# Two attention stages of a hybrid decoder block rewritten as deeper software pipelines, and the bodies of the expert loop in another order

## The reference

```
h = RMSNorm(x);  P = h @ W_mix_in        # conv u, B, C | diff q, k, v | memory q
conv   : B * causal_dwconv3(C * u)                                   256 channels
diff   : (softmax(q1 k1/8 + b) - lam * softmax(q2 k2/8 + b)) v       4 heads, causal, v 128 wide
         then RMSNorm per head
memory : softmax(q km/8) vm over 256 fixed tokens                     4 heads of 64
x = x + concat(conv, diff, memory) @ W_mix_out
x = x + MoE(RMSNorm(x))                  # top 4 of 32 experts, clamped SwiGLU, width 1024
out = RMSNorm(x)
```

## Time and profile before

| | |
|---|---|
| time, 3 runs | 2342.4 us median (2339.67 to 2343.84) |
| the profiled execution | 2346.0 us, its span 2344.4 us |
| PE busy | 2175.7 us, 93% |
| DVE busy | 1559.5 us, 67% |
| ACT busy | 1337.9 us, 57% |
| mean granted clock of TensorE | 0.966 |

### The profile page before, as it was taken

One profiled execution on the slowest core, in us unless ns is written; L12 is line 12 of the kernel. 1 busy time (PEld: TensorE's weight loads), 2 busy tenths in 40 slices (PEclk: granted clock), 3 DMA queues, 4 the chain that ended last, 5 costly groups with the idle time before them and its releaser, 6 DMA issues.

```text
span 2344.4 us, 34502 instructions
## 1 busy us (share of the span) xinstructions
PE 2175.7 (93%) x10770; PEld 1797.6 (77%) x10771; DVE 1559.5 (67%) x1640; ACT 1337.9 (57%) x1523; POOL 341.2 (15%) x306
## 2 busy tenths in 40 slices
PE   7999868799499999999999999999999999999993
PEld 6889645599388878877887878778888878888873
DVE  4411256655577658677866888987666888667754
ACT  5111247733366557566746777775556777556654
POOL 1000000012302002011201122121221222122100
PEclk9999979999699999999999999999999999999997
DMA  5111200052679669689968999997776999667854
GB/s 192 55 54 54 90 1 1 25 192 100 200 233 324 218 190 379 229 287 319 379 215 288 361 359 370 362 372 251 226 239 227 322 371 358 222 222 249 302 161 161
DMA packets 265288, 536.93 MB, mean 229 GB/s; under 512 B 14478, under 2 KB 31144, under 8 KB 265132
## 3 DMA queue, kind: packets, MB, share of 16 engines
q1 hardware_dynamic: 248332, 488.26, 58.8%
q0 software_dynamic: 16896, 47.83, 8.4%
HBM read 499.29 MB, written 36.75 MB: 229 GB/s over the span
## 4 chain that ended last, share of the span: by engine, by line
PE 69%; issue 7%; DVE 6%; ACT 3%; DMA 1%; POOL 0%; DVEq 0%; ACTq 0%; SPq 0%; POOLq 0%
PE ps L686 65%; ACT hT_hi L1146 1%; PE ps L911 1%; PE ps L918 1%; DVE work L1400 1%; PE ps L832 1%; DVE hT_lo L1565 1%; DVE w_lo L1554 1%; ACT region_mem L1181 0%; DVE work L1605 0%; DVE hT_lo L1575 0%; ACT hT_lo L1194 0%; DVE weight_ring L1681 0%; DVE slots_between L1554 0%; DVE d_lam L1397 0%
## 5 line engine op out<-in xcount | busy, mean ns | idle before, releaser
L686 PE MATMUL ps<-hT_hi,hT_lo 128*128 128x512 f32 (+1 forms) x4304 | 1399.1, 389 | 12.4 <-DVE hT_lo L1575 12.4
L686 PEld LDWEIGHTS ps<-hT_hi,hT_lo 128*128 128x128 f32 x4304 | 808.5, 189 | 183.3 <-DVE w_lo L1554 18.3
L1146 ACT ACTIVATE hT_hi<-weight_ring 128x2048 fp32r<-128x2048 f32 x417 | 786.9, 1914 | 195.7 <-PE ps L686 142.0
L1554 DVE TENSOR_TENSOR slots_between<-weight_ring,hT_hi 128x2048 fp32r<-128x2048 f32 x245 | 552.7, 2285 | 140.3 <-ACT hT_hi L1146 139.7
L686 PE MATMUL ps<-slots_between,hT_lo 128*128 128x512 f32 x1344 | 527.1, 392 | 0.0
L1554 DVE TENSOR_TENSOR w_lo<-weight_ring,hT_hi 128x2048 fp32r<-128x2048 f32 x140 | 319.5, 2283 | 33.7 <-ACT hT_hi L1146 33.7
L686 PE MATMUL ps<-w_lo,hT_lo 128*128 128x512 f32 (+1 forms) x896 | 336.1, 375 | 0.0
L686 PEld LDWEIGHTS ps<-slots_between,hT_lo 128*128 128x128 f32 x1344 | 254.4, 189 | 54.2
L686 PEld LDWEIGHTS ps<-w_lo,hT_lo 128*128 128x128 f32 x896 | 168.7, 188 | 30.3
L607 POOL DMA_INDIRECT residual_rows<-work,idx_now x48 | 119.0, 2478 | 475.7 <-ACT work L1207 284.8
L601 POOL DMA_INDIRECT work<-normed_rows,idx_far x49 | 86.7, 1770 | 457.4 <-PE ps L911 293.8
(11 more groups left out here) (251 smaller groups left out, 2468.4 us busy)
## 6 DMA issues: line engine op xcount, KB each, us to landing
weight_ring<-in_w_gate_up SPq DMA_DIRECT2D x280, 1024.0 KB, 7.3
weight_ring<-in_w_down SPq DMA_DIRECT2D x140, 1024.0 KB, 5.6
weight_ring<-in_w_mix_in SPq DMA_DIRECT2D x10, 1024.0 KB, 5.9
weight_ring<-in_x SPq DMA_DIRECT2D x8, 512.0 KB, 8.0
weight_ring<-in_w_mix_out SPq DMA_DIRECT2D x4, 1024.0 KB, 5.3
work<-in_x SPq DMA_DIRECT2D x8, 512.0 KB, 4.7
residual_rows<-work SPq DMA_DIRECT2D x8, 512.0 KB, 3.3
normed_rows<-work SPq DMA_DIRECT2D x8, 512.0 KB, 3.6
```

The lines of the kernel that those rows point to most:

```text
L686: return pe.matmul(o, l, r, start=first, stop=last)
L1146: act.activation(w_high_part(u), ring[:, home(u), :], ACT.Copy).then_inc(s["w_high_made"], 1)
L1554: dve.tensor_tensor(w_low_part(u), ring[:, home(u), :], w_high_part(u).bitcast(f32), ALU.subtract)\
```

## The change

Three things, in one version.

1. *Memory stage.* On DVE the normalising of a step goes one step back (maxima of i, then normalise i-1, copy i-2, copy out i-3). PE: scores i, transposes i-2, value product i-3. ACT: copy i-2 first, then the exponentials of i. The loops have one step more.
2. *Diff stage.* DVE: both score maps of j (side 1 first, `SIDES = (1, 0)`), then the difference of j-1. PE: scores j, transposes j-2, value product j-3. ACT: copy j-2, both exponentials of j, then output and square of j-3. The waits between the two stages are put off to where the buffer in question is first used. The square root over the head norms is made in two parts: 28 columns at j = 32, once the squares up to step 29 are through, the last 4 at the end.
3. *Expert loop.* `by_size` tests the other way round, so that the one-block body stands first, the body for two full blocks last.

```
 def by_size(eng, size, body):
-    with eng.If(size > P + 1):
-        with eng.If(size > P + SHORT + 1):
+    with eng.If(size < P + 2):
+        body(("full",))
+    with eng.Else():
+        with eng.If(size < P + SHORT + 2):
+            body(("full", "short"))
+        with eng.Else():
             body(("full", "full"))
-        with eng.Else():
-            body(("full", "short"))
-    with eng.Else():
-        body(("full",))
...
 # PE, diff stage
-            for j in range(NU + 2):
+            for j in range(NU + 3):
                 if j < NU:
-                    for c in range(2):
+                    for at, c in enumerate(SIDES):
                         if j >= 1:
-                            pe.wait_ge(s["ds_read"], 2 * j - 1 + c)
+                            pe.wait_ge(s["ds_read"], 2 * j - 1 + at)
...
-                if 1 <= j <= NU:
-                    n = j - 1
+                if 2 <= j < NU + 2:
+                    n = j - 2
                     pe.wait_ge(s["ds_diff"], n + 1)
...
 # ACT, diff stage
+                if 2 <= j < NU + 2:
+                    n = j - 2
...
                 if j < NU:
                     exponentials(j, 0)
-                if j >= 2:
-                    n = j - 2
+                    exponentials(j, 1)
+                if j >= 3:
+                    n = j - 3
...
+                if j in (NU, NU + 2):
+                    heads = slice(0, NU - HEADS) if j == NU else slice(NU - HEADS, NU)
+                    act.wait_ge(s["ds_sq"], j - 2)
+                    act.activation(o_std[:, heads], o_ssq[:, heads], ACT.Sqrt, ...).then_inc(s["o_std_made"], 1)
...
 # DVE, memory stage: one step back
-                    dve.wait_ge(s["ms_exp"], 4 * (i + 1))
-                    link(dve.reciprocal(m_inv[:, i % 2, :], m_sum[:, i % 2, :]))
+                    j = i - 1
+                    dve.wait_ge(s["ms_exp"], 4 * (j + 1))
+                    link(dve.reciprocal(m_inv[:, j % 2, :], m_sum[:, j % 2, :]))
...
 # DVE, diff stage
                 if j >= 2:
-                    dve.wait_ge(s["ds_turned"], j - 1)
+                    dve.wait_ge(s["ds_turned"] if c == 0 else s["ds_diff"], j - 1)
...
                 if j < NU:
                     scores_read(j, 0)
+                    scores_read(j, 1)
                 if j >= 1:
                     difference(j - 1)
-                if j < NU:
-                    scores_read(j, 1)
```

More of the change, by code:

```diff
@@ L766, in _ @@
             pe.wait_ge(s["proj_dve"], NG // 2)
-            for i in range(NT + 2):
+            for i in range(NT + 3):
                 if i < NT:
@@ L785, in _ @@
                     last.then_inc(s["ms_turned"], 1)
[L786 to L787 removed]
+                if i >= 3:
+                    j = i - 3
                     pe.wait_ge(s["ms_t_act"], j + 1)
@@ L816, in _ @@
                         last.then_inc(s["ds_done"], 1)
-                if j >= 2:
+                if 2 <= j < NU + 2:
                     n = j - 2
+                    pe.wait_ge(s["ds_diff"], n + 1)
+                    if n >= 1:
+                        pe.wait_ge(s["ds_t_act"], n)
+                    else:
+                        pe.wait_ge(s["ms_t_act"], NT)
+                        pe.wait_ge(s["ms_t_dve"], NT)
+                    for b in range(n // HEADS + 1):
+                        last = pe.transpose(ps[:, 4 + b // 4, P * (b % 4):P * (b % 4) + P], wk[:, 2 * (n % 2), P * b:P * b + P], ident[:, :])
+                    last.then_inc(s["ds_turned"], 1)
+                if j >= 3:
+                    n = j - 3
                     i, h = divmod(n, HEADS)
@@ L822, in _ @@
                         pe.wait_ge(s["ds_out"], n - 1)
+                    else:
+                        pe.wait_ge(s["ms_out"], NT)
                     for b in range(i + 1):
@@ L825, in _ @@
                     last.then_inc(s["ds_av"], 1)
-                if 1 <= j <= NU:
-                    n = j - 1
[L828 to L836, removed]
+            pe.wait_ge(s["ds_t_act"], NU)
             pe.wait_ge(s["wo_split"], 16)
@@ L1047, in _ @@
             act.activation(lam[:, 2:4], lam[:, 0:2], ACT.Exp).then_inc(s["lam_exp"], 1)
-            for i in range(NT + 1):
+            for i in range(NT + 2):
+                if i >= 2:
+                    j = i - 2
+                    act.wait_ge(s["ms_turned"], j + 1)
+                    if j >= 2:
+                        act.wait_ge(s["ms_av"], j - 1)
+                    act.activation(wk[:, 2 + j % 2, 0:512], ps[:, 4, :], ACT.Copy).then_inc(s["ms_t_act"], 1)
                 if i < NT:
@@ L1077, in exponentials @@
                     .then_inc(s["ds_exp"], 1)
-            for j in range(NU + 2):
+            for j in range(NU + 3):
+                if 2 <= j < NU + 2:
+                    n = j - 2
+                    nb = n // HEADS + 1
+                    act.wait_ge(s["ds_turned"], n + 1)
+                    if n >= 2:
+                        act.wait_ge(s["ds_av"], n - 1)
+                    act.activation(wk[:, 4 + n % 2, 0:P * nb], ps[:, 4:6, :].rearrange("p b n -> p (b n)")[:, 0:P * nb], ACT.Copy)\
+                        .then_inc(s["ds_t_act"], 1)
                 if j < NU:
                     exponentials(j, 0)
-                if j >= 2:
-                    n = j - 2
+                    exponentials(j, 1)
+                if j >= 3:
+                    n = j - 3
                     i, h = divmod(n, HEADS)
```

61 lines of the change are left out of this document (24 added, 37 removed).

## The result

| | median of 4 runs | range |
|---|---|---|
| kernel before | 2343.1 us | 2339.67 to 2345.58 |
| changed kernel | 2271.45 us | 2267.76 to 2272.37 |

A forecast was written before the change was run, and what follows sets the result against it. Expert loop bound by PE, attention stages by engines waiting for each other in turn. Terms -14 - 24 - 3 - 10 = -51 took 2346.0 to 2295.0, less 3.6 for the median: 2291 us, range 2276 to 2316.

The forecast's parts named there:

- D: Expert loop: reordering the bodies removes four of PE's five long idle times, -10 us, bounds -16 and +16.
- B: Diff stage: reading both maps before the previous step's difference brings steps to their busiest engine, -24 us, bounds -15 and -30.
- A: Memory stage: normalising one step back removes DVE's wait for exponentials, -14.0 us, bounds -5 and -17.
- C: Joint to the e stage: splitting the root takes table load and norm out of the chain, -3 us, bounds 0 and -4.
- the 1.5 and the 0.5: Memory stage: charges of 1.5 us for the longer loop and later last products, 0.5 us for the low clock at the start.
- a full clock: First twelve diff steps: at full clock ACT's 27.0 us is the bound, 30 us with joints, -11.4 us.
- the low-clock bound: First twelve diff steps: if the clock stays low, PE's busy 35.11 us is the bound, -6.3 us.
- The longer drain: Diff stage: filling and draining the longer pipeline, with one value product put ahead of the last, costs +1.5 us together.
- 1: Short diff steps and memory stage: the clock stays low, gains shrink to -8 and -19, 2302 us; chance 0.15.
- 2: Diff stage: side 0's read, waiting for transposes of step j-2, replaces the removed wait, 22 us back, 2313 us; chance 0.10.
- 3: Expert loop: the idle times only change place and the reordering gives 0, 2301 us; chance 0.12.
- 4: Expert loop: every one-block item pays for its two jumps, 79 us at 3.60 each, 2380 us; chance 0.05.

The follow-up runs named there:

- bodies_only: The kernel before with only the bodies of the expert loop in the new order: 2325.7 us, ratio 0.9908.
- sides_0_1: The changed kernel with side 0 read first in the diff stage: 2289.7 us, ratio 0.9760.
- after_pad64: The changed kernel with the expert loop shifted by 32 instructions in PE's program, by long-fulfilled waits ahead of it: 2317.6 us, ratio 0.9880.
- filler kernel: The changed kernel with 128 additional products of the identity on PE where it waits, into an unread bank: 2271.2 us, ratio 0.9685.

## Why the prediction was wrong

The forecast was 20 us too high. Of the 74.9 us between the spans it had 51. The missing 23.9 are 11.8 in D, 8.3 in B, 4.2 in A and 0.9 in C, less the 1.3 that the start lost. Either of D and B at its forecast size would have put the time inside the range. The low end of the range was also narrower than its own words: D and B at the bounds named there give 2291 - 6 - 4 = 2281, and all four bounds together some 2275.

- **A, memory stage: right in mechanism, mis-sized.** 18.2 instead of 14. The step is 3.61 us, not 3.75, since DVE's joints are shorter than I allowed: 8 x (5.75 - 3.61) = 17.1. The rest of the stage, for which I charged 2.0 us (the 1.5 and the 0.5), became 1.1 us shorter instead; the granted clock between 280 and 288 us was 0.79 instead of 0.50. My own bound was -17.
- **B, diff stage: the failing step is the floor.** "Each step should come down to its busiest engine" took PE's busy time at 768, 896 and 1024 keys. The steps came in below it: 15.49 for 16.31, 17.18 for 18.52, 4.54 for 5.10 a step. What bounds them is DVE's and ACT's work (16.89 and 16.77 of 17.18 at 896 keys). But ACT's busy time in the earlier trace rows was no floor either: at 512 and 640 keys I took 11.82 and 14.69, and the steps came to 11.29 and 13.90. Only DVE's figures in these rows (9.84, 13.86, 15.44, 17.00) lie below all four. A busy time read in steps full of waits came out too long on PE and on ACT. The four long stretches gave -3.9, -3.65, -4.4 and -5.1 where I had -3.4, -2.9, -3.6 and -3.7; the end of the differences -5.7 for -3.0. The first twelve steps gave -11.4 for -9. That is the size I gave to a full clock, yet the clock was 0.77: the low-clock bound, PE's 35.11 us as a floor, failed as above. The longer drain cost 1.8 us (start of the last difference to the end of the last square 6.46, now 8.27) for the 1.5 charged, but for another reason than the one given: the table load and the first root now stand in the chain ahead of the last copy (L1090), 1.6 us (from 409.27 to 410.88, in the chain that ended last):

```profile
409.31 1.26 issue
410.57 0.32 ACT o_std L1112
410.88 0.92 ACT work L1090
```

- **C, joint: right in size, in part by the choice of the border.** 3.9 for 3, inside its bounds. The table load of 1.28 us was not hidden, as I had it, but moved in front of the last square, where it is B's drain that pays for it. Drain and joint together gave 2.1 us.
- **D, expert loop: right only in sign, and the reason I gave falls.** All parts of it together gave 21.8, as bodies_only does on its own (21.6), against 10. First the sum: the idle times ahead of items 4, 7, 12 and 34 gave back 3.76, 2.19, 3.31 and 2.23 us by the starts of neighbouring matmuls, 11.5 for my 10.9, the one at item 8, which I left out, 4.3; behind four of the five TensorE ran at 0.50 for a few us, 1.7 to 1.9 us each, which I did not count at all; ahead of item 0 another 6.1 went, whose idle time of 8.44 us, the longest of the loop, does not hold (so 29 starts, not 30, had no such idle time). Items 0 and 1 took back 7.1: a new idle time ahead of item 1 and its low clock. Then the reason: "that body runs into the end by itself" is not what freed them. Shifted by 32 instructions the same order loses 46 us. The 21.8 us are thus the luck of this place: in the places at 32, 64, 96 and 127 the same change takes 2304 to 2318 us, 13 to 27 above my forecast.
- **Rivals.** 1: the clock did stay low in part of the short steps. It can hardly have mattered much: ACT was busy for 7.95 of 10 us in that spell, which leaves at most 3 of its 14 us (an estimate), and no run has these steps at the full clock. 2: real, but covered; sides_0_1 gives it 20 us. 3: not in this place of the loop; at 32, 64, 96 and 127 the idle times do change place, and cost more than they did before. 4 was the case nearest to what can happen: in the bad places the new order takes 32 to 46 us more than in the good one. Who pays is another than I had it. In after_pad64 the starts at items 4, 7 and 34 stand behind items of two full blocks, and those at 6 and 11, with 7.30 and 5.55 us the longest after item 0, are starts of such items behind an item of one block; no start of a one-block item behind another pays there. It needed the loop's size against what PE keeps, and I argued from order only.
- **Where it could be read before.** The queue's packets in the kernel before: 43, of which 12 came after item 2 had started, and 8 of these after item 4 had, when the loop had been through all three bodies. Packets that come again say that the loop does not fit, and then a change of PE's program anywhere ahead of it can move the time. Of these packets had two; "not much else of the loop had any" was wrong, and I took the two as a mark of the jump, not of the size.

What the prediction gave as signs: DVE's wait for exponentials gone, steps under 4 us, 512-key steps under 3.0 (11.29/4 = 2.82), clock in the short steps above 0.63: all came true. That no idle time over 2 us stands behind a two-block item is true for two full blocks, but behind item 0, a full and a short block, there is one of 3.01. The stage lengths, 37 and 115 us, were 32.9 and 107.6.

## What to carry to other kernels

A busy time read in steps full of waits is no safe floor: that of PE, which is modelled, came out up to 1.3 us too long for four steps and that of ACT up to 0.8, that of DVE not at all. See whether the same work has ever been done in less. In a software pipeline, put the read whose buffer is the last to come free behind another piece of work; its order alone was worth 20 us here. Before crediting a gain or loss in a device loop to an edit, count the packets of the program queue after all bodies have run once, and shift the loop by a few dozen instructions: a gain in one place that is a loss in the next is luck. A smaller loop was the cure in the one place where it was tried. And count in the trace how many instructions a shift really adds: for the float32 products here it was twice what I had assumed, and by the wrong count the good places seemed scattered.

## What was not expected of the hardware

- The time of a loop of 1716 TensorE instructions depends on its place in the program: 1519 to 1554 us for the same 32 items, by shifts of 32 instructions that cost nothing. At the worst of these places a loop of 1523 instructions kept one start with an idle time of over 2 us after item 0, not six.
- An idle time of 2 to 5 us on PE in the expert loop cost another 1.7 to 1.9 us of low clock after it, but not each did. Behind that of 2.04 us, which ended at 1016.24 in the kernel before, the clock stayed at 1.00; behind that of 2.08 us, at 2271.21, it fell. The stretches (columns as in the earlier trace rows):

```profile
1014.00:1022.00 8.00, 5.96 (x26) 4.80 (x26) 2.82 (x2) 5.11 (x4) 1.66 (x1) 1.00 0.86 206
2272.00:2278.00 6.00, 6.00 (x22) 4.78 (x22) 2.32 (x2) 3.34 (x2) 0.91 (x1) 0.79 0.84 197
```

- TensorE was granted 0.50 for 14 us while PE was shown busy for 98% ahead of it and in it (filler kernel), in steps of 64-row score products and short transposes. The Trainium skill ("TensorE: Matmul & The Clock Gate", What's actually happening) has it that activity releases the clock. By PE's busy time as the trace has it this spell does not agree with that rule; whether that busy time is the activity meant, and which property of this work is behind the spell, no run here shows.
